# A depthwise convolution whose taps move to TensorE as products over token phases

## The chip, the cores and the metric

The kernel runs on one core of a Trainium2 chip. Its time is the device time of one execution in microseconds. All data are fp32, and the large matrix products are made from a high and a low part in fp32r, three products for one.

## What is computed

The model has eight stages on 512 tokens of 1024 channels: two attention layers, then feed-forward, S5, feed-forward, feed-forward, **convolution**, feed-forward. Only the convolution mixer changes:

```
def layernorm(x, g, b):
    mu = mean(x); var = mean((x - mu)^2)          # over the 1024 channels
    return (x - mu) * rsqrt(var + EPS) * g + b

def conv_mixer(h, w_in, b_in, dw, dw_b, ln_g, ln_b, w_out, b_out):
    z = h @ w_in + b_in                           # 1024 -> 2048
    a, g = split(z, 2)
    z = a * sigmoid(g)
    z = depthwise_conv(z, dw, causal, 31 taps) + dw_b
    z = silu(layernorm(z, ln_g, ln_b))
    return z @ w_out + b_out
```

Every output token of a channel is a sum over 31 earlier tokens of the same channel, with 31 weights of its own.

## The kernel before

Channels lie on the 128 partitions in eight tiles (KD = 8), tokens along the free dimension (T = 512). Each stage is five functions, one for each engine's queue (SP issues the DMAs; PE, ACT, DVE and POOL compute), ordered by semaphores. An engine works its queue strictly in the written order, so a wait holds up all that is behind it.

Weights come in blocks of 256 columns into two slots. `load_block` (L364) waits until the block two before has been split; `split_h` on ACT makes the high part once PE is done with the slot (`mm_done`), `split_l` on DVE the low part (two inputs in SBUF, 128x2048), and then PE may start (`l_done`). `mm3` makes the three products. Each of the four passes `i` of the convolution's input projection uses two blocks, b0+2i (the value half, banks 0 and 1) and b0+2i+1 (the gate half, banks 2 and 3), and gives the tiles 2i and 2i+1: 48 matmuls of 512 columns for a block. `in_pair` is the first pass, tangled with the end of the stage before.

DVE evicts the banks with the factor `rstd` (L1226 and L1233: one operand in PSUM), ACT takes the sigmoid (L1166), and DVE multiplies both (L1237) into `ZP`, which has 30 zero columns ahead of the tokens. The taps of a tile are then divided. On PE (`taps_pe`, L1110) a tap is a product with a diagonal matrix: ACT makes two diagonals for a tap (high and low, L1181) and PE three products of 512 columns, 14 taps for a tile, 17 for the last two. On DVE (`taps_dve`, L1123) a tap is one multiply-add over 512 columns, `CV = CV + w * shifted ZP`, followed by a drain since the next one reads what it wrote. One tap is in ACT's first copy (L1173). `merge` (L1217) adds the bank to `CV`. PE makes the taps of pass i-1 after the projection of pass i. POOL makes the low parts of `ZP` (L1267).

The layer norm follows in one line: POOL sums the eight tiles (L1274), PE sums over partitions with a matrix of ones (L1144), ACT scales the mean (L1185), DVE subtracts it from each tile (L1249), ACT squares (L1190), POOL sums (L455), PE sums over partitions (L1146), ACT takes the root (L1192), DVE the reciprocal (L1251) and the product (L1254), ACT Silu (L1196) and the high part (L1199), DVE the low part (L1257). With the first low part PE begins the output projection (`out_pe`).

Of the kernel before, what the change touches and what calls it, by code (L numbers as in the profile page):

```python
# [7 lines left out]
ALU = mybir.AluOpType  # L8
ACT = mybir.ActivationFunctionType
# [86 lines left out]
def program(nc, io, stages=FULL):  # L96
    ctx = ExitStack()
    with ctx:
# [128 lines left out]
        ZP = sb("ZP", [P, KD, CONV_PAD + T], F32, rb)  # L227
        CV = sb("CV", [P, KD, T], F32, rb)
        SG = sb("SG", [P, 2, T], F32, rb)
        ZH = sb("ZH", [P, KD, CONV_PAD + T], F32R, rb)  # L230
        ZL = sb("ZL", [P, KD, CONV_PAD + T], F32R, rb)
        dwH = sb("dwH", [P, CONV_W * KD], F32R, rb)
        dwL = sb("dwL", [P, CONV_W * KD], F32R, rb)
        DIAGS = 30
        diag = sb("diag", [P, DIAGS, P], F32R, rb)
        YC = ZP[:, :, 0:T]
# [73 lines left out]
        def col(name, k, n=0):  # L310
# [14 lines left out]
            "s5": dict(z=KD, h2=KD, l2=KD, ysq_in=8, ysq_use=6),  # L325
# [768 lines left out]

        def conv_sp(sp, s):
            b0 = first_block[s]
            w = io["cv_w_in_2"][0].rearrange("(k p) n -> p k n", p=P)
            for i in range(4):
                load_block(sp, b0 + 2 * i, 0, raw3(0, KD), w[:, :, i * 256:(i + 1) * 256])
                load_block(sp, b0 + 2 * i + 1, 1, raw3(1, KD), w[:, :, D + i * 256:D + (i + 1) * 256])  # L1100
            out_sp(sp, b0 + 8, io["cv_w_out_2"][0])

        def share(k):
            return 17 if k >= KD - 2 else 14

        TAPS_P = [sum(share(k) for k in range(n)) for n in range(KD + 1)]

        def taps_pe(pe, s, k):  # L1110
            n, acc = share(k), bank[4 + k % 3][:, :]
            pe.wait_ge(ss(s, "zl"), at(s, "zl", k + 1))
            if k >= 3:
                pe.wait_ge(ss(s, "cv"), at(s, "cv", k - 2))
            for t in range(n):
                d = 2 * (TAPS_P[k] + t)
                pe.wait_ge(ss(s, "diag"), at(s, "diag", d + 2))
                high, low = diag[:, d % DIAGS, :], diag[:, (d + 1) % DIAGS, :]
# [4 lines left out]
        def taps_dve(dve, k, t0, t1):  # L1123

            for t in range(t0, t1):
                dve.scalar_tensor_tensor(CV[:, k, :], ZP[:, k, t:t + T], dwT[:, t * KD + k:t * KD + k + 1],  # L1126
                                         CV[:, k, :], ALU.mult, ALU.add)
                dve.drain()

        def conv_pe(pe, s):  # L1130
            b0, j0 = first_block[s], tiles_before[s]
            for i in range(4):
                if i == 0:
                    in_pair(pe, s, b0, j0)
                    continue
                pe_block256(pe, b0 + 2 * i, 0, j0 + 4 * i, XH, XL)
                pe_block256(pe, b0 + 2 * i + 1, 1, j0 + 4 * i + 2, XH, XL)
                if i >= 1:
                    taps_pe(pe, s, 2 * i - 2)
                    taps_pe(pe, s, 2 * i - 1)  # L1140
            taps_pe(pe, s, KD - 2)
            taps_pe(pe, s, KD - 1)
            pe.wait_ge(ss(s, "cvsum"), at(s, "cvsum", KD))
            pe.matmul(stat[:, :], ones[:, :], ssq[:, :], start=True, stop=True).then_inc(ss(s, "cvstat"), 1)  # L1144
            pe.wait_ge(ss(s, "censum"), at(s, "censum", KD))
            pe.matmul(stat[:, :], ones[:, :], ssq[:, :], start=True, stop=True).then_inc(ss(s, "censtat"), 1)  # L1146
            out_pe(pe, s, b0 + 8, j0 + 16, (s, "l2"))

        def conv_act(act, s):
# [6 lines left out]
            act.activation(dwH[:, :], dwT[:, :], ACT.Copy).then_inc(ss(s, "dwh"), 1)  # L1156
            act.wait_ge(ss(s, "dwl"), at(s, "dwl", 1))

            for i in range(4):
# [9 lines left out]
                for k in (2 * i, 2 * i + 1):  # L1169
                    act.wait_ge(ss(s, "z"), at(s, "z", k + 1))  # L1170
                    act.activation(ZH[:, k, :], ZP[:, k, :], ACT.Copy).then_inc(ss(s, "zh"), 1)
                    last = CONV_W - 1
                    act.activation(CV[:, k, :], ZP[:, k, last:last + T], ACT.Identity, bias=col("cv_dw_b_2", k),  # L1173
                                   scale=dwT[:, last * KD + k:last * KD + k + 1]).then_inc(ss(s, "cva"), 1)
                for k in (2 * i, 2 * i + 1):
                    for t in range(share(k)):
                        n = TAPS_P[k] + t
                        if 2 * n >= DIAGS:
                            act.wait_ge(ss(s, "ptap"), at(s, "ptap", n - DIAGS // 2 + 1))
                        for m, part in enumerate((dwH, dwL)):  # L1180
                            act.activation(diag[:, (2 * n + m) % DIAGS, :], ident[:, :], ACT.Copy,  # L1181
                                           scale=part[:, t * KD + k:t * KD + k + 1].bitcast(F32))\
                               .then_inc(ss(s, "diag"), 1)
            act.wait_ge(ss(s, "cvstat"), at(s, "cvstat", 1))
            act.activation(rms[:, :], stat[:, :], ACT.Copy, scale=1.0 / D).then_inc(ss(s, "mu"), 1)  # L1185
            for k in range(KD):
# [1313 lines left out]
```

## Time and profile before

| | |
|---|---|
| time, median of 3 runs | 3062.64 us (3060.99 to 3070.03) |
| the profiled execution | 3068.31 us, of which span 3066.5 us |
| busy: PE, DVE, ACT, POOL | 91%, 54%, 38%, 15% of the span |
| the chain that ended last | PE 76%, DVE 10%, issue 4%, ACT 3% |
| convolution stage | from about 2403 to 2699 us on the profile's clock |
| its taps | PE and DVE, from 2439 to 2585 us |
| its layer norm | to 2622 us |
| mean granted TensorE clock | 0.938 of full speed |

The page tells the share of each engine over the whole span and in 40 slices of 77 us. The convolution fills under four of these, so it is read from questions put to the trace: busy time in stretches, an engine's instructions in order of time, and the groups of instructions of one line. In a row of a timeline the first number is the start in us, the second the length; "x8" behind it means eight instructions merged into one row, from the first start to the last end. A bracket gives the idle time of the engine before it, and what ended it.

### The profile page before, as it was taken

What the parts mean: (1) busy time and instruction counts of PE and PEld (TensorE: products, weight loads), DVE (VectorE), ACT (ScalarE), POOL (GpSimd) and SP (SyncE); (2) the same over time, 40 slices, a digit from 0 to 9 for tenths busy, and PEclk for the clock granted to TensorE, in tenths of its full rate; (3) what the DMA queues carried; (4) which work ended last, traced back from release to release, by engine and by line L of the source; (5) the groups of instructions that cost most, each with busy time, mean ns of one, the idle gap of its engine ahead of it and who ended that gap; (6) DMA issues with size and microseconds to landing.
All of it is one profiled execution on the core that took longest, in us unless ns stands there. A gap on an engine that the chain in (4) does not pass through costs nothing.

```text
span 3066.5 us, 37070 instructions
## 1 busy us (share of the span) xinstructions
PE 2799.9 (91%) x13972; PEld 2299.9 (75%) x13972; DVE 1653.3 (54%) x2427; ACT 1156.3 (38%) x1943; POOL 449.2 (15%) x383
## 2 busy tenths in 40 slices
PE   6987978978979999989699999999999997899998
PEld 5855767845768888888578888888888885788887
DVE  4469755379756543375536443264432697554423
ACT  3237843237834432222324222242222565432222
POOL 1011001020017830024302000010000212200000
PEclk9987989987999999987699999999999998899999
DMA  3320002220014332342222222332223210123222
GB/s 129 96 82 1 1 28 85 97 68 1 1 34 119 132 117 82 99 133 70 64 81 81 85 95 84 95 97 84 94 84 94 83 56 28 56 83 96 87 87 74
DMA packets 292400, 234.80 MB, mean 77 GB/s; under 512 B 43683, under 2 KB 286060, under 8 KB 291756
## 3 DMA queue, kind: packets, MB, share of 16 engines
q1 hardware_dynamic: 289180, 219.49, 23.5%
q10 hardware_dynamic: 2016, 7.46, 0.8%
q0 software_dynamic: 1072, 6.10, 0.6%
q8 instruction: 82, 1.34, 0.2%
q14 instruction: 50, 0.41, 0.0%
HBM read 220.83 MB, written 12.19 MB: 76 GB/s over the span
## 4 chain that ended last, share of the span: by engine, by line
PE 76%; DVE 10%; issue 4%; ACT 3%; DVEq 3%; POOLq 2%; POOL 1%; SPq 0%; DMA 0%; ACTq 0%
PE bank L376 23%; PE bank L378 22%; PE bank L377 22%; DVE WL L362 2%; PE bank L1566 1%; ACT WH L357 1%; DVE stats L1870 1%; PE bank L1553 1%; PE bank L1578 1%; DVE XL L434 1%; DVE CV L1126 1%; POOLq L2318 1%; DVEq L1871 1%; POOLq L2316 1%; DVE E L1897 1%
## 5 line engine op out<-in xcount | busy, mean ns | idle before, releaser
L376 PE MATMUL bank<-XH,WH 128*128 128x512 f32 (+1 forms) x2688 | 996.8, 371 | 79.2 <-DVE WL L362 25.4
L378 PE MATMUL bank<-XH,WL 128*128 128x512 f32 (+1 forms) x2688 | 988.4, 368 | 0.0
L377 PE MATMUL bank<-XL,WH 128*128 128x512 f32 (+1 forms) x2688 | 986.7, 367 | 0.0
L362 DVE TENSOR_TENSOR WL<-raw,WH 128x2048 fp32r<-128x2048 f32 (+1 forms) x212 | 447.8, 2112 | 558.1 <-ACT WH L357 557.7
L376 PEld LDWEIGHTS bank<-XH,WH 128*128 128x128 f32 x2688 | 516.6, 192 | 176.6 <-issue 37.5
L357 ACT ACTIVATE WH<-raw 128x2048 fp32r<-128x2048 f32 (+1 forms) x212 | 370.0, 1746 | 581.6 <-PE bank L378 581.6
L377 PEld LDWEIGHTS bank<-XL,WH 128*128 128x128 f32 x2688 | 517.3, 192 | 90.0 <-issue 1.0
L378 PEld LDWEIGHTS bank<-XH,WL 128*128 128x128 f32 x2688 | 516.1, 192 | 87.8
L378 PE MATMUL bank<-HH,WL 128*128 128x512 f32 (+1 forms) x792 | 293.4, 371 | 0.0
L376 PE MATMUL bank<-HH,WH 128*128 128x512 f32 (+1 forms) x792 | 293.3, 370 | 0.0
L377 PE MATMUL bank<-HL,WH 128*128 128x512 f32 (+1 forms) x792 | 292.7, 370 | 0.0
L976 POOL TENSOR_TENSOR ssq<-ssq,sq 128x512 f32<-128x512 f32 x24 | 31.0, 1292 | 1195.8 <-ACT sq L887 1195.8
L844 ACT ACTIVATE HH<-work 128x512 f32 (+1 forms) x88 | 55.7, 632 | 362.4 <-DVE work L930 362.4
L377 PEld LDWEIGHTS bank<-HL,WH 128*128 128x128 f32 x792 | 148.9, 188 | 28.8
L376 PEld LDWEIGHTS bank<-HH,WH 128*128 128x128 f32 x792 | 148.6, 188 | 28.2
L378 PEld LDWEIGHTS bank<-HH,WL 128*128 128x128 f32 x792 | 148.8, 188 | 27.6
L840 ACT ACTIVATE work<-work 128x512 f32<-128x512 f32 x88 | 55.2, 632 | 270.5 <-DVE work L923 270.5
L928 DVE TENSOR_TENSOR work<-bank,rstd 128x512 f32<-128x512 f32 x88 | 60.8, 690 | 171.7 <-PE bank L378 167.8
L923 DVE TENSOR_TENSOR work<-bank,rstd 128x512 f32<-128x512 f32 x88 | 60.1, 687 | 163.6 <-PE bank L378 154.2
L1712 ACT ACTIVATE E<-bank,stats 128x512 f32<-128x512 f32 (+1 forms) x176 | 113.1, 646 | 47.6 <-DVE stats L1872 36.0
L1870 DVE TENSOR_REDUCE stats<-bank 128x1 f32<-128x512 f32 (+1 forms) x176 | 107.7, 634 | 28.7 <-PE bank L1555 27.5
L1566 PE MATMUL bank<-ident,E 128*128 128x128 f32 x448 | 82.8, 308 | 34.2 <-DVE PTL L1879 31.0
(379 smaller groups left out, 3599.8 us busy)
## 6 DMA issues: line engine op xcount, KB each, us to landing
raw<-in_ffn_w_dram SPq DMA_DIRECT2D x88, 1024.0 KB, 5.3
raw<-in_ffn_w_dram SPq DMA_DIRECT2D x64, 704.0 KB, 4.6
raw<-in_w_in_dram SPq DMA_DIRECT2D x24, 1024.0 KB, 5.2
raw<-in_w_out_dram SPq DMA_DIRECT2D x8, 1024.0 KB, 5.1
raw<-in_cv_w_in_dram SPq DMA_DIRECT2D x8, 1024.0 KB, 5.4
cs_scr<-CSA ACTq DMA_DIRECT2D x8, 520.0 KB, 3.0
raw<-in_w_mem_kv_dram SPq DMA_DIRECT2D x4, 1024.0 KB, 5.4
raw<-in_s_w_in_dram SPq DMA_DIRECT2D x4, 1024.0 KB, 7.7
```

The source lines that it names most:

```text
L357: act.activation(WH[:, slot, 0:n * P], raw[:, slot, 0:n * P], ACT.Copy).then_inc(h_done, 1)
L362: dve.tensor_tensor(WL[:, slot, 0:n * P], raw[:, slot, 0:n * P], WH[:, slot, 0:n * P].bitcast(F32), ALU.subtract).then_inc(l_done, 1)
L376: pe.matmul(out, WH[:, slot, c:c + P], h, start=start, stop=False)
L377: pe.matmul(out, WH[:, slot, c:c + P], l, start=False, stop=False)
L378: return pe.matmul(out, WL[:, slot, c:c + P], h, start=False, stop=stop)
L840: act.activation(work2[:, o, :], work1[:, o, :], ACT.Silu).then_inc(ss(s, "silu"), 1)
L844: act.activation(HH[:, bass.ds(2 * i + o, 1), :], work1[:, o, :], ACT.Copy).then_inc(ss(s, "hh"), 1)
L923: dve.tensor_tensor(work1[:, o, :], bank[o][:, :], rstd[:, :], ALU.mult).then_inc(acc_read, 1)
L928: dve.tensor_tensor(work1[:, o, :], bank[2 + o][:, :], rstd[:, :], ALU.mult).then_inc(acc_read, 1)
L1566: mm = pe.transpose(bank[4 + u % 2][:, c * P:(c + 1) * P], E[:, SCORE0[u] % 6, c * P:(c + 1) * P], ident[:, :])
L1712: act.activation(E[:, m % 6, 0:nk * P], bank[m % 4][:, 0:nk * P], ACT.Exp, bias=stats[:, 1, m % 8:m % 8 + 1], scale=scale, accum_out=stats ...
L1870: dve.tensor_reduce(stats[:, 0, c:c + 1], bank[(m + i) % 4][:, 0:nk * P], AX, ALU.max)
```

## The change

Tiles 0, 1 and 2 (`TILES_D`) stay on DVE, with all of their 31 taps there (one in ACT's first copy, 30 on DVE). Tiles 0 and 1 are done in turns, with a drain only after each pair; `CHUNKS` spreads the 90 taps over the four passes as 14, 16, 16 and 44.

Tiles 3 to 7 (`TILES_P`) go to PE whole. The tokens of such a tile are split in four phases (token = 4n + phase) and its channels in four groups of 32. The gate product is written in phase order into `ZS`; 16 DMAs of 32 partitions x 128 tokens bring it to `PZ`, where the 128 partitions are 4 phases x 32 channels. There the convolution of one group is nine products of 128 rows, 128 output rows and 128 columns, in plain fp32, summed in PSUM: 36 for a tile. Their weight matrices `MM` are made by POOL, half a tile in one operation: the tap table `WT` (broadcast along 32 columns) times a 32x32 identity `EYE` (broadcast along 72), 128x2304 elements out, ten such products in three buffers. ACT fills `WT` and `EYE` with 20 small copies first. A finished tile is evicted by ACT into `PO`, goes back with 16 DMAs into `CP`, and ACT copies it with the bias into `CV`. The 160 DMAs are issued by SP, between the loads of weights.

The layer norm takes a provisional mean from the five tiles that are ready first (0, 1, 3, 4, 5: POOL's sum, then PE and ACT), subtracts it from each tile as the tile comes, squares it on ACT and sums over partitions on PE for each tile. PE also sums the last three centred tiles; that gives the mean that is left, which is taken out of the variance and then out of the tiles (four on DVE, four on POOL). Root and reciprocal become a logarithm and an exponential on ACT. The sum of the provisional mean stands ahead of tile 7's products on PE, and on ACT tile 7's eviction stands behind the first five squares.

The diff, cut to its core:

```diff
@@ taps and queues
+        TILES_D = (0, 1, 2)
+        TILES_P = (3, 4, 5, 6, 7)
+        FIRST = (0, 1, 3, 4, 5)
+        CENTRE = FIRST + (2, 6, 7)
+        TAPS_D = [(k, t) for t in range(CONV_W - 1) for k in (0, 1)] + [(2, t) for t in range(CONV_W - 1)]
+        CHUNKS = (0, 14, 30, 46, len(TAPS_D))
...
         def conv_sp(sp, s):
+            def to_phases(k):
+                n = k - TILES_P[0]
+                sp.wait_ge(ss(s, "z"), at(s, "z", k + 1))
+                if n >= 1:
+                    sp.wait_ge(ss(s, "u_in"), at(s, "u_in", 16 * PH * 4 * n))
+                for g in range(4):
+                    for ph in range(PH):
+                        sp.dma_start(PZ[ph * PW_:(ph + 1) * PW_, n, g, LEAD:], ZS[g * PW_:(g + 1) * PW_, k % 2, ph, :])\
+                          .then_inc(ss(s, "u_in"), 16)
+            def from_phases(k):
+                n = k - TILES_P[0]
+                sp.wait_ge(ss(s, "po"), at(s, "po", n + 1))
+                if n >= 1:
+                    sp.wait_ge(ss(s, "y_out"), at(s, "y_out", 16 * PH * 4 * n))
+                for g in range(4):
+                    for ph in range(PH):
+                        q = PH - 1 - ph
+                        sp.dma_start(CP[g * PW_:(g + 1) * PW_, n, ph, :], PO[q * PW_:(q + 1) * PW_, n % 2, g, :])\
+                          .then_inc(ss(s, "y_out"), 16)
+            for i in range(3):
+                pair(i)
+            to_phases(3)
+            pair(3)
+            to_phases(4)
+            to_phases(5)
+            out_block(0)
+            out_block(1)
+            to_phases(6)
+            to_phases(7)
+            for k in (3, 4, 5):
+                from_phases(k)
+            out_block(2)
+            out_block(3)
+            for k in (6, 7):
+                from_phases(k)
@@ conv_pe
-                pe.matmul(acc, high, ZH[:, k, t:t + T], start=(t == 0), stop=False)
-                pe.matmul(acc, high, ZL[:, k, t:t + T], start=False, stop=False)
-                pe.matmul(acc, low, ZH[:, k, t:t + T], start=False, stop=(t == n - 1)).then_inc(ss(s, "ptap"), 1)
+            for half in range(2):
+                m = 2 * n + half
+                pe.wait_ge(ss(s, "diag"), at(s, "diag", m + 1))
+                for g in (2 * half, 2 * half + 1):
+                    for j in range(9):
+                        c = (g % 2) * NQ + j * PH
+                        mm = pe.matmul(acc[:, g * NS:(g + 1) * NS],
+                                       MM[:, m % 3, c:c + PH, :].rearrange("p q c -> p (q c)"),
+                                       PZ[:, n, g, j:j + NS], start=(j == 0), stop=(j == 8))
+                mm.then_inc(ss(s, "ptap"), 1)
...
+                if i == 2:
+                    taps_pe(pe, s, 3)
+            for k in (4, 5, 6):
+                taps_pe(pe, s, k)
+            pe.wait_ge(ss(s, "cvsum"), at(s, "cvsum", len(FIRST)))
+            pe.matmul(stat[:, :], ones[:, :], ssq[:, :], start=True, stop=True).then_inc(ss(s, "cvstat"), 1)
+            taps_pe(pe, s, 7)
+            for n, k in enumerate(CENTRE):
+                if k not in FIRST:
+                    pe.wait_ge(ss(s, "cen"), at(s, "cen", n + 1))
+                    mm = pe.matmul(bank[6][:, :], ones[:, :], CV[:, k, :], start=(n == len(FIRST)), stop=(n == KD - 1))
+                pe.wait_ge(ss(s, "censq"), at(s, "censq", n + 1))
+                pe.matmul(stat[:, :], ones[:, :], sq[:, n % 2, :], start=(n == 0), stop=(n == KD - 1))\
+                  .then_inc(ss(s, "censtat"), 1)
@@ conv_act
-            act.activation(dwH[:, :], dwT[:, :], ACT.Copy).then_inc(ss(s, "dwh"), 1)
-                        for m, part in enumerate((dwH, dwL)):
-                            act.activation(diag[:, (2 * n + m) % DIAGS, :], ident[:, :], ACT.Copy,
+            for ph in range(PH):
+                rows = slice(ph * PW_, (ph + 1) * PW_)
+                act.activation(EYE[rows, :], ident[rows, rows], ACT.Copy)
+                for g in range(4):
+                    ins = act.activation(WT[rows, :, g, 5 - ph:5 - ph + CONV_W], taps[g * PW_:(g + 1) * PW_, TILES_P[0]:, :],
+                                         ACT.Copy)
+            ins.then_inc(ss(s, "wt"), 1)
...
+            evict(3)
+            evict(4)
+            back(3)
+            evict(5)
+            back(4)
+            evict(6)
+            back(5)
             act.wait_ge(ss(s, "cvstat"), at(s, "cvstat", 1))
+            act.activation(rms[:, :], stat[:, :], ACT.Copy, scale=1.0 / (P * len(FIRST))).then_inc(ss(s, "mu"), 1)
+            for n in range(len(FIRST)):
+                square_c(n)
+            evict(7)
+            square_c(5)
+            back(6)
+            square_c(6)
+            back(7)
+            square_c(7)
@@ conv_dve
+            def taps(i):
+                for n in range(CHUNKS[i], CHUNKS[i + 1]):
+                    k, t = TAPS_D[n]
...
+                    ins = dve.scalar_tensor_tensor(CV[:, k, :], ZP[:, k, t:t + T], dwT[:, t * KD + k:t * KD + k + 1],
+                                                   CV[:, k, :], ALU.mult, ALU.add)
...
+                    if k:
+                        dve.drain()
...
+            for n in range(KD):
+                centre(n)
+            dve.wait_ge(ss(s, "mu"), at(s, "mu", 2))
+            dve.wait_ge(ss(s, "censtat"), at(s, "censtat", KD))
+            dve.scalar_tensor_tensor(work2[:, 0, :], stat[:, :], 1.0 / D, work1[:, 1, :], ALU.mult, ALU.subtract)\
+               .then_inc(ss(s, "var"), 1)
+            for k in range(4):
+                dve.tensor_tensor(CV[:, k, :], CV[:, k, :], work1[:, 0, :], ALU.subtract)
@@ conv_pool
+            def matrices(m):
+                n, half = m // 2, m % 2
+                shape = [P, 2 * NQ, PW_]
+                if m >= 3:
+                    pool.wait_ge(ss(s, "ptap"), at(s, "ptap", m - 2))
+                w = WT[:, n, 2 * half:2 * half + 2, :].rearrange("p g q -> p (g q)")
+                pool.tensor_tensor(MM[:, m % 3], w.unsqueeze(2).to_broadcast(shape),
+                                   EYE[:, :].unsqueeze(1).to_broadcast(shape), ALU.mult).then_inc(ss(s, "diag"), 1)
...
+            for m in range(8):
+                matrices(m)
+            add(0)
+            add(1)
+            matrices(8)
+            add(2)
+            add(3)
+            matrices(9)
+            add(4)
+            pool.wait_ge(ss(s, "mu"), at(s, "mu", 2))
+            for k in range(4, KD):
+                pool.tensor_tensor(CV[:, k, :], CV[:, k, :], work1[:, 0, :], ALU.subtract).then_inc(ss(s, "csub"), 1)
```

## Rows read from the trace of the kernel before

**Rows 1.** busy time by stretch: us, then busy us (count) per engine, clock, DMA

```profile
2431.00:2584.70 153.70, 149.99 (x642) 120.53 (x642) 136.11 (x161) 102.64 (x268) 28.20 (x14) 1.00 0.16 51
2584.70:2615.10 30.40, 4.15 (x5) 1.03 (x5) 18.69 (x20) 13.65 (x19) 12.94 (x9) 0.51 0.00 0
```

**Rows 2.** DVE's timeline, 2551 to 2585: start, us, engine, line, operation, count, idle

```profile
2551.58 1.28 DVE L1233 TENSOR_TENSOR work<-bank,rstd 128x512 f32<-128x512 f32 x2
...
2557.68 1.28 DVE L1219 TENSOR_TENSOR CV<-CV,bank 128x512 f32<-128x512 f32 x2
2558.88 24.96 DVE L1126 SCALAR_TENSOR_TENSOR CV<-ZP,dwT,CV 128x512 f32<-128x512 f32 x26
2583.92 1.29 DVE L1219 TENSOR_TENSOR CV<-CV,bank 128x512 f32<-128x512 f32 x2
```

**Rows 3.** timelines of PE, DVE and ACT in the layer norm

```profile
2587.41 2.08 PE L1144 MATMUL bank<-ssq,ones 128*128 128x512 f32 x2 [4.39 <-POOL ssq L1274]
...
2611.55 0.80 ACT L1196 ACTIVATE CV<-CV,vecT 128x512 f32<-128x512 f32 x1
...
2612.92 0.80 ACT L1196 ACTIVATE CV<-CV,vecT 128x512 f32<-128x512 f32 x1
...
2621.25 0.69 DVE L1257 TENSOR_TENSOR XL<-CV,XH 128x512 fp32r<-128x512 f32 x1 [0.68 <-ACT XH L1199]
```

**Rows 4.** timelines of ACT and DVE at the start of the convolution

```profile
2429.59 0.40 ACT L1156 ACTIVATE dwH<-dwT 128x248 fp32r<-128x248 f32 x1
2432.39 1.28 ACT L1166 ACT_TABLE_LOAD   x1 [2.39 <-DVE work L1233]
...
2434.44 1.41 DVE L1237 SCALAR_TENSOR_TENSOR ZP<-work,vecT,SG 128x512 f32<-128x512 f32 x2 [1.53 <-ACT SG L1166]
2436.86 2.29 DVE L362 TENSOR_TENSOR WL<-raw,WH 128x2048 fp32r<-128x2048 f32 x1 [1.00 <-ACT WH L357]
```

**Rows 5.** PE's timeline: starts at full clock, and eight fp32 records of 128 columns

```profile
2441.15 0.39 PE L376 MATMUL bank<-XH,WH 128*128 128x512 f32 x1
...
2442.08 0.39 PE L377 MATMUL bank<-XL,WH 128*128 128x512 f32 x1
...
2428.01 1.05 PE L478 MATMUL bank<-ident,rcol 128*128 128x128 f32 x8
```

**Rows 6.** granted clock of a stretch, and two starts inside it

```profile
2615.00:2619.00 4.00, 3.90 (x9) 3.15 (x10) 2.94 (x5) 3.90 (x7) 0.00 (x0) 0.50 0.00 0
...
2615.66 0.63 PE L377 MATMUL bank<-XL,WH 128*128 128x512 f32 x1
2616.09 0.63 PE L378 MATMUL bank<-XH,WL 128*128 128x512 f32 x1
```

**Rows 7.** timelines of POOL and DVE in an earlier feed-forward stage

```profile
964.55 1.95 POOL L738 TENSOR_TENSOR tabA<-tabA,par 128x1024 f32<-128x1024 f32 x1
966.45 4.00 POOL L739 TENSOR_TENSOR tabA<-tabA,par 128x1024 f32<-128x1024 f32 x1
...
965.22 3.43 DVE L362 TENSOR_TENSOR WL<-raw,WH 128x2048 fp32r<-128x2048 f32 x1 [2.50 <-ACT WH L357]
968.57 0.68 DVE L928 TENSOR_TENSOR work<-bank,rstd 128x512 f32<-128x512 f32 x1
969.33 1.65 DVE L930 TENSOR_TENSOR work<-work 128x512 f32<-128x512 f32 x1
```

**Rows 8.** DVE's timeline in the centring, and the first tap

```profile
2592.56 1.75 DVE L1249 TENSOR_TENSOR CV<-CV,rms 128x512 f32<-128x512 f32 x1
...
2439.07 1.85 DVE L1126 SCALAR_TENSOR_TENSOR CV<-ZP,dwT,CV 128x512 f32<-128x512 f32 x1
```

**Rows 9.** POOL's product of two plain inputs of 1024

```profile
973.22 2.40 POOL L742 TENSOR_TENSOR tabA<-tabA,bt 128x1024 f32<-128x1024 f32 x1
```

**Rows 10.** SyncE's timeline in the s5 stage, and its DMA issues by line

```profile
1342.66 3.88 SPq L1980 DMA_DIRECT2D u_scr<-sq  x8
...
y_scr<-YS SPq DMA_DIRECT2D x64, 32.0 KB, 1.9
```

More of the change, by code:

```diff
@@ L1097, in conv_sp, with pair @@
             w = io["cv_w_in_2"][0].rearrange("(k p) n -> p k n", p=P)
-            for i in range(4):
+            wo = io["cv_w_out_2"][0].rearrange("(k p) n -> p k n", p=P)
+            def pair(i):
                 load_block(sp, b0 + 2 * i, 0, raw3(0, KD), w[:, :, i * 256:(i + 1) * 256])
                 load_block(sp, b0 + 2 * i + 1, 1, raw3(1, KD), w[:, :, D + i * 256:D + (i + 1) * 256])
-            out_sp(sp, b0 + 8, io["cv_w_out_2"][0])
-        def share(k):
-            return 17 if k >= KD - 2 else 14
@@ L1123, in taps_dve, with out_block @@
[L1123 to L1128, printed above, removed]
+            def out_block(i):
+                load_block(sp, b0 + 8 + i, i % 2, raw3(i % 2, KD), wo[:, :, i * 256:(i + 1) * 256])
+            def to_phases(k):
[7 more added lines that the diff above has]
+                          .then_inc(ss(s, "u_in"), 16)
@@ L1184, in conv_act @@
-            act.wait_ge(ss(s, "cvstat"), at(s, "cvstat", 1))
-            act.activation(rms[:, :], stat[:, :], ACT.Copy, scale=1.0 / D).then_inc(ss(s, "mu"), 1)
-            for k in range(KD):
-                act.wait_ge(ss(s, "cen"), at(s, "cen", k + 1))
-                if k >= 2:
-                    act.wait_ge(ss(s, "censum"), at(s, "censum", k - 1))
-                act.activation(square_to(k), CV[:, k, :], ACT.Square).then_inc(ss(s, "censq"), 1)
-            act.wait_ge(ss(s, "censtat"), at(s, "censtat", 1))
@@ new lines, in conv_act @@
+            square_c(7)
+            act.wait_ge(ss(s, "censum"), at(s, "censum", 1))
+            act.activation(work1[:, 0, :], bank[6][:, :], ACT.Copy, scale=1.0 / D)
+            act.activation(work1[:, 1, :], bank[6][:, :], ACT.Square, scale=1.0 / D).then_inc(ss(s, "mu"), 1)
+            act.wait_ge(ss(s, "var"), at(s, "var", 1))
+            act.activation(work2[:, 0, :], work2[:, 0, :], ACT.Ln, bias=eps_c[:, 0:1]).then_inc(ss(s, "sigma"), 1)
+            act.wait_ge(ss(s, "sigma"), at(s, "sigma", 1))
@@ L1258, in conv_dve @@
                    .then_inc(ss(s, "l2"), 1)
+            for k in range(KD):
+                if k >= 4:
+                    dve.wait_ge(ss(s, "csub"), at(s, "csub", k - 3))
+                dve.tensor_tensor(CV[:, k, :], CV[:, k, :], rms[:, :], ALU.mult).then_inc(ss(s, "nrm"), 1)
+                if k >= 2:
+                    low(k - 2)
+            low(KD - 2)
+            low(KD - 1)
             out_dve(dve, s, b0 + 8, j0 + 16, s0 + 16, YC, post, lambda o: col("cv_b_out_2", o))
@@ new lines, in add @@
+            def add(n):
+                k = FIRST[n]
+                if k in TILES_D:
+                    pool.wait_ge(ss(s, "cv"), at(s, "cv", k + 1))
+                else:
+                    pool.wait_ge(ss(s, "cvb"), at(s, "cvb", k - TILES_P[0] + 1))
+                if n == 0:
+                    ins = pool.tensor_copy(ssq[:, :], CV[:, k, :])
+                else:
+                    ins = pool.tensor_tensor(ssq[:, :], ssq[:, :], CV[:, k, :], ALU.add)
+                ins.then_inc(ss(s, "cvsum"), 1)
+                pool.wait_ge(ss(s, "cvsum"), at(s, "cvsum", n + 1))
```

174 lines of the change are left out of this document (87 added, 87 removed).

## The prediction

> **What bounds the kernel now.** I read the page first, then busy time by stretch, then the timelines of DVE, ACT and PE around the convolution, and last the chain of waits behind it. All times below are on the clock of the profiled execution before (span 3066.5 us, 3068.3 us in all); the median of its runs is 3062.6, and I put differences on that median. The page shows PE busy for 91% of the span, so elsewhere in the kernel nothing that this change touches can matter. In the convolution there are two stretches [rows 1]. From 2431 to 2585 PE (150 of 154 us) and DVE (136) are both full: TensorE does 118 taps as three fp32r products each, VectorE 122 taps at 0.83 us each and the evictions [rows 2]. From 2585 to 2615 PE does 4 us of work: that is the layer norm's serial chain, sum, mean, centring, squares summed on POOL, root, reciprocal, and then a 1.37 us rhythm of Silu and copy on ACT [rows 3]. The next matmuls need the eight lows of the result; the last is ready at 2621.25 + 0.69 = 2621.9. From there both kernels do the same work, so the question is: when is that eighth low ready afterwards?
>
> **Matmuls.** TensorE loses 354 products of 0.233 us (four starts in 0.93 [rows 5]), 82.5 us. It gains five tiles of 36 fp32 products of 128 columns. Eight instruction records of just that shape take 1.05 us [rows 5]: at most 0.131 from start to start, and 0.111 when the last one's tail is taken off, which I use. An fp32 product leaves two records, so a tile is 72 x 0.111 = 8.0 us (9.4 at most) and the five are 40. After 10 us of PE idle time the granted clock was 0.50 of full speed (1.2 GHz) for the 4.0 us from 2615 on, with 0.43 us between starts instead of 0.233 [rows 6]: such a return costs some 1.9 us.
>
> **VectorE's own work.** 122 taps and 8 merges become 90 taps. Tiles 0 and 1 alternate and drain once per pair. Two undrained operations of this kind start 0.66 us apart (1.41 - 0.75 [rows 4]), a drained one takes 0.83, so 30 pairs cost 44.7 and tile 2 24.8: some 70 us, against 107.
>
> **The shared port, the term that decides.** POOL now makes ten weight products of 128x2304 with both inputs read in SBUF. What such an operation does to DVE is seen far from here: while POOL's L738 (128x1024, one input broadcast) ran from 964.55, a split on DVE that began at 965.22 took 3.43 us instead of 2.29; L739, issued at 966.45, then took 4.00 instead of 1.95; and L930 behind it 1.65 instead of 0.69. The DVE eviction between them, with one operand in PSUM, took its usual 0.68 [rows 7]. So two-SBUF-input work on DVE and work on POOL exclude each other, an instruction at a time. They take turns: in the centring DVE operations take 1.75 us, 1.06 of it a wait for POOL's 512-element sum; the first tap took 1.85 in place of 0.75 [rows 8]. The Trainium skill (SBUF — State Buffer, Who interferes with whom) has the rule behind it, that a DVE instruction with two SBUF inputs and a GpSimd instruction that reads SBUF exclude each other and the later one "fully blocks". By that rule, which speaks against this change, a tap waits for a whole product; were the port only shared out, the sum would be nearer the first rival below. The trace agrees with the rule (3.43 and 1.65 us).
>
> How long is one product? L739 held DVE until about 970.3, from 968.5, 1.8 us for 1024 elements [rows 7]. In proportion 2304 take 4.1 us, which I use: same kind, one input broadcast. The least is 3.8 (if part of the 1.8 is fixed). The most is from L742 with two plain inputs, 2.40 us of which some 0.1 is start-up, 2.25 x 2304/1024 = 5.1 [rows 9].
>
> **The start.** ACT's conversion of the taps (0.40 us [rows 4]) becomes 20 small copies of 32 partitions. At most 0.40 each is 8, at least 0.2 is 4; I take 6.0, ending 2435.7. POOL's first product starts there. The table load and two sigmoids follow (to 2438.3), and ACT's split of the second block of weights ends 2440.1. On DVE two gate operations and a split, all with two SBUF inputs, now take turns with three products: product to 2439.9, gate to 2440.6, product to 2444.7, gate to 2445.4, product to 2449.5, split to 2451.7. In the kernel before it ended at 2439.15 [rows 4], and PE needs it at 2431.3 + 48 x 0.233 = 2442.5. PE stalls 9.2 us and comes back at the lower clock, 1.9 more. VectorE then does 14 taps (10.4), two evictions and a split before the next pair can begin, 0.7 after PE is free. So the last of the projections ends at 2431.3 + 3 x 22.4 + 8.0 (tile 3) + 9.2 + 1.9 + 0.7 = 2518.3.
>
> **To the end of the taps.** From the evictions of that pair to the taps DVE needed 6.1 us (2551.58 to 2557.68 [rows 2]); so they start at 2524.4. 14 paired taps and 30 single ones are 10.4 + 24.8. Against them stand five products (5 to 9), each free to start only as PE uses up earlier ones, and five sums: 5 x 4.1 + 5 x 1.06 = 25.8. End: 2585.4, where before it was 2585.2 (2583.92 + 1.29 [rows 2]). So PE and DVE each lose about 40 us of work, and the port gives it back.
>
> **The queue of SyncE.** 160 transfers join it. Eight of the nearest kind are issued in 3.88 us, so 0.47 each, and land 1.9 us after [rows 10]: 16 are 7.6 + 1.8 = 9.4 us. Ahead of the loads of the output weights now stand tiles 4 and 5: the first load leaves near 2507 and lands 5.4 later, 2512.4, and DVE comes to its split near 2516. After gate 6 (2521) come tiles 6 and 7 out and 3, 4, 5 back, 45 us, to 2566; then a sum, the provisional mean, and tile 7 on PE, done near 2578. That hides under the taps with 14 us to spare counted to ACT's eviction of tile 7, because ACT does five squares first.
>
> **The tail.** After the last tap: centre and square 1.4, three sums of squares on PE, at the lower clock as L1144 had after 4 us idle (two records in 2.08 [rows 3], some 0.4 of it tail, so 1.7 us apart, later 1.4) 4.7, and the fifth square 0.5: 6.6. Eviction and 16 transfers: 9.6. Copy back, centre, two fp32 products at 1.7, variance: 5.6. Four subtractions on DVE in turns with POOL's four: 5.5, and they hide ACT's logarithm and exponential. Multiply, Silu, copy, low: 2.9; seven more at 1.37: 9.6. In all 39.8, against 2621.9 - 2585.2 = 36.7. The eighth low comes at 2625.2, 3.3 us later than before: 3066 us. With products of 3.8 to 5.1, copies of 4 to 8 us and a clock at either level throughout, the likeliest case spans -6 to +9: 3057 to 3072.
>
> **Rivals.** (1) The products cost DVE little, because POOL gets these broadcast reads through faster or DVE slips taps in. For it: DVE and PE have really lost 40 us of work; against it, rows 7 and 8. Without stalls the pairs end at 2507 and the taps near 2550, and SyncE becomes the bound: gate 6 at 2510.6, 45.2 us of transfers, 3.8 for copy, sum and mean, 9.9 for tile 7, 10.0 for its eviction and way back, then 5.6 + 2.4 + 2.9 + 9.6: 2600. That is 22 us less, 3041; at half the stalls, about 3050. (2) A product is as dear as a plain one, 5.1 us: three at the start and five at the end at 1.0 more each, and the tail unchanged: +8, 3074. It decides for slower from some 4.9 us a product. The Trainium skill (GPSIMD Engine Reference, Elementwise — side-by-side cycle accounting) gives 4497 ns for a plain 2048-element `tensor_tensor`; an estimate from that page is 5.06 us for 2304 and a time of 3074. (3) SyncE's queue is the bound: 80 transfers between gate 6 and the mean have 14 us to spare, so from 0.65 us a transfer. At 0.8 it is 80 x 0.15 + 16 x 0.33, some 17 us more, 3083. Rows 10 speak against it, but those transfers run to DRAM, these from one partition group of SBUF to another.
>
> **Chances.** A measurement can tell about 0.3%, 9 us: faster is below 3053.4, slower above 3071.8. Likeliest case 0.52 (0.05 faster, 0.43 same, 0.04 slower); rival 1 0.22, all faster; rival 2 0.18 (0.03 same, 0.15 slower); rival 3 0.08 (0.02 same, 0.06 slower). Faster 0.27, same 0.48, slower 0.25. The range reaches to most of rivals 1 and 2 and leaves out about 0.1 on each side: 3045 to 3079.
>
> **What would show it.** Right: product records on POOL of 4 us and more; about five taps of some 4.9 us on DVE; the second block of the projections 9 us late with a granted clock of half behind it; the last tap near 2585; ACT's eviction of tile 7 after the fifth square. Rival 1: taps all near 0.8, PE waiting for POOL's sum before tile 7. Rival 2: products of 5 us or more. Rival 3: SyncE issuing without a pause beyond 2580, and copies back late. What would make it wrong: a product time outside 3.8 to 5.1, DVE passing POOL twice in a row, or transfers that take another time than those to DRAM.

## The result, and the profile after

The change makes the kernel slower: 3088.6 us (median of 4 runs, 3084.3 to 3092.3) against 3064.6 for the kernel before on the same chip (3061.0 to 3070.0), a ratio of 1.0076 (1.0055 to 1.0097). The prediction was 3066, with 3079 as its upper end, and a chance of 0.25 for slower. The profiled execution took 3084.3 us, of which 3082.5 are span.

The start of the convolution moves by up to 13 us between executions of the same code in the stages before it, and from the eighth low part to the end every profiled execution takes 444.5 to 444.6 us. So every comparison below uses one measure inside the stage: from the start of ACT's `rstd` (2429.10 before, 2421.37 after) to the end of the eighth low part (2621.94 and 2637.97). Before it is **192.8 us**, after **216.6**: +23.8, where the medians differ by 24.0. Each such number comes from one profiled execution; the ratios come from all. Positions written "at 159" are us after the start of `rstd`.

Busy time after, in two stretches (us; busy us and count of PE, PEld, DVE, ACT, POOL; clock; DMA share; GB/s): from `rstd` to the last tap on DVE, and from there to the eighth low part.

```profile
2421.37:2580.70 159.33, 105.70 (x588) 90.73 (x586) 134.97 (x121) 35.39 (x46) 52.00 (x14) 0.84 0.17 52
2580.70:2637.97 57.27, 30.91 (x117) 18.47 (x117) 22.06 (x29) 26.56 (x36) 7.54 (x5) 0.76 0.16 48
```

PE is busy for 106 us of the first stretch where it was for 150 [rows 1], and DVE is nearly as full as it was (135 us busy, 136 before), through its turns with POOL: its last tap comes at 159.3 where the last merge before came at 156.1. So the first stretch costs 3 us and the second, 57.3 long where it was 36.7, costs 20.5. The second one is on DVE's timeline:

```profile
2576.66 4.04 DVE L1308 SCALAR_TENSOR_TENSOR CV<-ZP,dwT,CV 128x512 f32<-128x512 f32 x1 [0.43 <-issue]
2589.57 3.70 DVE L1352 TENSOR_TENSOR CV<-CV,rms 128x512 f32<-128x512 f32 x6 [8.87 <-ACT rms L1270]
2603.65 0.69 DVE L1352 TENSOR_TENSOR CV<-CV,rms 128x512 f32<-128x512 f32 x1 [10.37 <-ACT CV L1237]
2614.49 0.69 DVE L1352 TENSOR_TENSOR CV<-CV,rms 128x512 f32<-128x512 f32 x1 [10.14 <-ACT CV L1237]
2618.86 0.69 DVE L1359 SCALAR_TENSOR_TENSOR work<-bank,work 128x512 f32<-128x512 f32 x1 [3.68 <-PE bank L1205]
2619.47 5.92 DVE L1362 TENSOR_TENSOR CV<-CV,work 128x512 f32<-128x512 f32 x4
```

The taps are done and the mean is not there: 8.87 us. Then DVE waits twice for a tile on its way back. Three of the longest waits from 2425 us on (engine and line, what it waited for, us, times, longest):

```profile
ACT CV L1237 <- DMA CP<-PO: 60.9, 4, 33.3
...
PE bank L1196 <- POOL ssq L1406: 37.2, 1, 37.2
...
ACT WH L360 <- DMA raw<-in_cv_w_out_dram: 26.7, 1, 26.7
```

TensorE stood 37.2 us before tile 7 for GpSimd's sum, the sum stood for ACT's copies back, and those for their transfers. SyncE's timeline says why:

```profile
2463.29 10.11 SPq L1134 DMA_DIRECT2D PZ<-ZS  x16
2473.44 1.21 SPq L371 DMA_DIRECT2D raw<-in_cv_w_in_dram  x2
2487.71 22.32 SPq L1134 DMA_DIRECT2D PZ<-ZS  x32
2510.07 1.21 SPq L371 DMA_DIRECT2D raw<-in_cv_w_out_dram  x2
2528.47 21.76 SPq L1134 DMA_DIRECT2D PZ<-ZS  x32
2550.27 32.78 SPq L1146 DMA_DIRECT2D CP<-PO  x48
2583.09 1.21 SPq L371 DMA_DIRECT2D raw<-in_cv_w_out_dram  x2
2584.40 27.62 SPq L1146 DMA_DIRECT2D CP<-PO  x32
```

16 transfers take 10.11 us to issue, 0.63 each, where [rows 10] had 0.47. From 2528.5 to 2583.1 SyncE issues set after set; the only pauses, up to 1.3 us, are for the set before to land. The load of block b0+8 leaves only at 2510.07, at 88.7, behind the transfers of tiles 4 and 5; ACT waits 26.7 us for it. So gate 6 (the product of value and gate half of tile 6, L1324) starts at 103.6 and, in turns with a product of POOL, ends at 107.1.

### The profile page after: what moved, and what is told of

Read it like the earlier page. It is cut to its first block, busy times and chain, and to the rows that moved or that the text cites. A ratio compares the mean times of both kernels' runs of the same rounds, so it can differ in the third digit from the quotient of the medians.

```text
span 3082.5 us, 36962 instructions
## 1 busy us (share of the span) xinstructions
PE 2768.4 (90%) x13998; PEld 2274.3 (74%) x13998; DVE 1653.5 (54%) x2390; ACT 1094.8 (36%) x1727; POOL 469.5 (15%) x381
## 4 chain that ended last, share of the span: by engine, by line
PE 72%; DVE 10%; issue 4%; ACT 4%; DVEq 3%; SPq 3%; POOLq 2%; DMA 1%; POOL 1%; ACTq 0%
PE bank L379 21%; PE bank L380 21%; PE bank L381 21%; DVE WL L365 2%; SPq L1134 2%; PE bank L1710 1%; ACT WH L360 1%; SPq L1146 1%; DVE stats L2014 1%; PE bank L1697 1%; DVE XL L437 1%; PE bank L1722 1%; DVE work L534 1%; DVE X L538 1%; POOLq L2462 1%
## 5 line engine op out<-in xcount | busy, mean ns | idle before, releaser
L365 DVE TENSOR_TENSOR WL<-raw,WH 128x2048 fp32r<-128x2048 f32 (+1 forms) x212 | 459.7, 2169 | 561.4 <-ACT WH L360 561.0
L448 POOL TENSOR_TENSOR ssq<-ssq,sq 128x256 f32<-128x256 f32 x112 | 96.4, 860 | 118.4 <-ACT sq L428 112.8
```

What stands on the lines that cost most here:

```text
L365: dve.tensor_tensor(WL[:, slot, 0:n * P], raw[:, slot, 0:n * P], WH[:, slot, 0:n * P].bitcast(F32), ALU.subtract).then_inc(l_done, 1)
L448: ins = pool.tensor_tensor(ssq[:, HALF[h]], ssq[:, HALF[h]], sq[:, k % 2, HALF[h]], ALU.add)
```

## The experiments

Two theories at the start. **Q**: two chains end almost together, VectorE's with the port lock, and SyncE's queue of transfers, and the queue is the later one. **L**: the port lock is the whole loss. The first kernel cuts the products to a ninth (of this and the next diffs only the core is shown):

```diff
-                shape = [P, 2 * NQ, PW_]
+                shape = [P, 8, PW_]
```

> The changed kernel with each of POOL's ten weight products cut from 128x2304 to 128x256 elements (the other weights stay zero, so the convolution of tiles 3 to 7 is left unfinished); everything else, the 160 transfers too, is as in the change. Measure: from the eviction of the first statistic (rstd) to the end of the eighth low, 192.8 us before and 216.6 after. Theory Q (two chains end almost together, SyncE's queue of transfers last): the three stalls by products go, gates 6 and 7 come some 13 us earlier and with them the sum ahead of tile 7, but PE still waits for that sum long after the taps are done; 14 us less, 202 to 203. Theory L (the port lock is the whole loss): 25 us less or more, 190, below the kernel before.

Measured: 199.9 us; ratio to before 1.0009 (0.9997 to 1.0021). With no long hold of the port left, the stage is still 7 us slower than before, where L wanted 190; Q had 202 to 203. The taps end 27 us earlier, at 132.1, and the same wait is longer:

```profile
2582.10 3.70 DVE L1352 TENSOR_TENSOR CV<-CV,rms 128x512 f32<-128x512 f32 x6 [19.61 <-ACT rms L1270]
```

L falls as the whole cause. The queue moves up by 17 us too, since the stall at the start and the turns of the splits delay the gates that feed it.

Loads ahead of transfers:

```diff
-            to_phases(4)
-            to_phases(5)
             out_block(0)
+            to_phases(4)
             out_block(1)
+            to_phases(5)
```

> The changed kernel with the load of the first output block ahead of tile 4's transfers and the second ahead of tile 5's, nothing else. Theory Q: the split that waited for the load until 2515.6 can begin some 6 us earlier, the last pass and gates 6 and 7 follow, and so does all of SyncE's chain: 7 us less, 209 to 211. Theory L: the taps on DVE stay where they were and the end moves by less than 2 us.

Measured: 205.6; ratio 1.0044 (1.0030 to 1.0057). 11.0 us come back for two loads moved, more than the 6 to 8 expected: gate 6 starts at 93.0 instead of 103.6, and what stands behind it moves up by 11 to 12.

The price of a transfer by itself, put into the kernel before (SyncE's timeline; in order: 32x512 B between SBUF buffers across groups of 32 partitions; the same within a group; to DRAM; to DRAM in pieces of 256 B while loads run; four of 64 KB; four of 128x512 B):

> The kernel before with six batches of transfers of scratch data on SyncE's queue during the projection (and 20 instead of 30 buffers for diagonals, to make room). It measures the disputed cost by itself: start to start of issues on SyncE. In the change it was 0.63 us for 32 partitions x 512 bytes from SBUF to SBUF, against 0.47 for the S5 stage's SBUF to DRAM. If it is the crossing of partition groups, only the first batch shows 0.63; if it is SBUF as the target, the first two, the batch of four-times-larger and of 128 partitions too; if it is the shape of 32 rows of 512 bytes, the batch to DRAM with this shape too, and the one in S5's shape (16 rows in eight pieces of 256 bytes) 0.47.

```profile
2424.61 10.36 SPq L1114 DMA_DIRECT2D PB<-PA  x16
2436.19 10.66 SPq L1120 DMA_DIRECT2D PB<-PA  x16
2448.07 7.31 SPq L1126 DMA_DIRECT2D p_scr<-PA  x16
...
2456.52 9.00 SPq L1133 DMA_DIRECT2D q_scr<-PA  x16
2466.93 2.61 SPq L1139 DMA_DIRECT2D PB<-PA  x4
2472.22 2.48 SPq L1144 DMA_DIRECT2D PB<-PA  x4
```

0.65 and 0.67 us each from SBUF to SBUF, crossing or not; 0.46 to DRAM, 0.56 there in small pieces beside loads; and 0.65 and 0.62 from SBUF to SBUF for four times the bytes. The dear ones have SBUF at both ends, whatever their size up to 64 KB. Which end costs is not shown: the transfers from DRAM into SBUF in the kernel with the hop by way of DRAM, below, lasted 0.34 to 0.60 us each.

Returns issued by ACT instead of SyncE (the `sp.` calls of `from_phases` become `act.`, each set behind its eviction):

> The changed kernel with the 80 returning transfers issued by ACT behind each eviction, and the 80 outgoing ones still by SyncE. Theory Q: the returns of tiles 3 and 4 no longer queue behind tiles 6 and 7, the sum ahead of tile 7 comes some 13 to 20 us earlier, then the end of the taps on DVE (2580.7) is what the first centring waits for: 5 to 9 us less, 208 to 212. Theory L: 2 us less at most.

Measured: 214.9; ratio 1.0051 (1.0032 to 1.0070). The expected 208 to 212 were missed. ACT's timeline shows one cause:

```profile
2541.52 10.36 ACTq L1219 DMA_DIRECT2D CP<-PO  x16
2551.93 0.60 ACT L1227 ACTIVATE PO<-bank 128x512 f32<-128x512 f32 x1 [10.44 <-issue]
2553.13 11.89 ACTq L1219 DMA_DIRECT2D CP<-PO  x16
```

ACT pays the same price, and its next eviction and copy stand behind it for 10 us. The other cause is chance. Gate 6, which this edit does not reach, came 4 us later, because gate 4 began 0.5 us later (65.6 against 65.1), met a product of POOL and took 4.9 us in place of 1.2. The gates of tiles 4 and 5, in after and here:

```profile
2486.46 6.11 DVE L1324 SCALAR_TENSOR_TENSOR ZS<-work,vecT,SG 128x512 f32<-128x512 f32 x2 [0.19 <-ACT SG L1253]
...
2496.64 9.81 DVE L1325 SCALAR_TENSOR_TENSOR ZS<-work,vecT,SG 128x512 f32<-128x512 f32 x2 [0.19 <-ACT SG L1249]
```

So a single stage number of a kernel with POOL's products can be off by some 4 us. The returns of tile 3 are still 6 us earlier (at 134) and the mean 4.6. The ratio, whose interval overlaps after's, doesn't settle what this edit is worth.

Light products and loads first, together:

> After with both of the edits of the two kernels before it: GpSimd's products are cut to 128x256 (most of the convolution of tiles 3 to 7 is left out: its matrices are wrong), and SyncE issues the load of block b0+8 ahead of tile 4's transfers and that of b0+9 ahead of tile 5's. Measured from the start of rstd to the end of the eighth low part, after takes 216.6 us, light products alone 199.9 (16.7 less), loads alone 205.6 (11.0 less). If the products and the transfer queue bind in the same places (the wait of the split of b0+8, the sixth gate), what both give together is less than the 27.8 us that they sum to: my reckoning of the queue gives 193 to 196 us (21 to 24 less). If they add up, 189. If the products were the only cause and the loads merely repaired what they had delayed, the loads add nothing: 199 to 200. Kernel: 193 to 196 is 3062 to 3067 us.

Measured: 195.9, inside the 193 to 196; ratio 1.0020 (1.0006 to 1.0033). The two gains of 16.7 and 11.0 make 20.7, not 27.8: both shorten one path, the one to gate 6. DVE's wait for the mean is still 20.11 us. With neither long products nor the loads in the way the stage is still 3 us slower than before, and the mean, which comes through the queue, is what DVE waits for.

The queue itself. Each set of 16 is replaced by four transfers to DRAM and one of 256 KB back:

```diff
-                    for ph in range(PH):
-                        sp.dma_start(PZ[ph * PW_:(ph + 1) * PW_, n, g, LEAD:], ZS[g * PW_:(g + 1) * PW_, k % 2, ph, :])
+                    sp.dma_start(z_scr[n, :, :, g].rearrange("q c s -> c q s"), ZS[g * PW_:(g + 1) * PW_, k % 2])
+                sp.wait_ge(ss(s, "u_in"), at(s, "u_in", HOP * n + 64))
+                sp.dma_start(PZ[:, n, :, LEAD:], z_scr[n].rearrange("q c g s -> (q c) g s"))
```

> After, with each set of 16 transfers replaced by four to a DRAM buffer and one of 256 KB back from it (same rows, same places), so SyncE issues 5 transfers for a tile in place of 16, products as they are. Theory Q (the issue of 16 transfers at 0.63 us, 10.1 us of SyncE a set, is what the end waits for): a set takes 4 x 0.46 + 0.65 of issue and 1.9 of landing in between, about 4.5 us, the load of b0+8 is issued about 11 us earlier, the fifth sum no longer ends last, the taps on VectorE do (they end 156 to 159 after rstd), evict 7 behind the five squares at 166, eighth low 198 to 200: 16 to 18 us less than after's 216.6, kernel 3068 to 3072. Theory L (the shared port alone): the products and their stalls stay, less than 4 us change. If the extra hop costs more than it saves (landing of 2 to 3 us twice for every tile on the path of gates 5 to 8), 216 or more.

Measured: 192.8; ratio 1.0004 (0.9991 to 1.0016). All 23.8 us are gone, more than the 16 to 18 expected, with every product and its lock still there. SyncE and DVE:

```profile
2463.27 1.79 SPq L1136 DMA_DIRECT2D z_scr<-ZS  x4
2466.41 0.60 SPq L1139 DMA_DIRECT2D PZ<-z_scr  x1
...
2515.05 1.79 SPq L1136 DMA_DIRECT2D z_scr<-ZS  x4
2518.18 0.53 SPq L1139 DMA_DIRECT2D PZ<-z_scr  x1
...
2575.55 0.75 DVE L1313 SCALAR_TENSOR_TENSOR CV<-ZP,dwT,CV 128x512 f32<-128x512 f32 x1 [0.43 <-issue]
2576.47 3.70 DVE L1357 TENSOR_TENSOR CV<-CV,rms 128x512 f32<-128x512 f32 x6 [0.16 <-DVE CV L1313]
```

An outgoing set takes 3.6 to 3.7 us with the hop, a returning one 3.4 to 7.1. Tile 7's way back, from SyncE's first issue to ACT's copy, takes 6.1 us where it took 11.3. The sum ends at 135, the centring follows the last tap after 0.16 us, and the last tap comes at 154.9. (The products only had other things to collide with: the split of b0+8 took 2.3 us here and 6.0 in after.)

To show that it is the issuing and not the route, eleven transfers that nobody uses are put in front of each set of five:

```diff
+                for j in range(11):
+                    g, ph = j // 4, j % 4
+                    sp.dma_start(PD[ph * PW_:(ph + 1) * PW_, g, 8:], ident[g * PW_:(g + 1) * PW_, :])
```

> The kernel with the hop by way of DRAM (f2, 192.8 us from rstd to the eighth low part against after's 216.6), with eleven transfers of 32x512 B from a constant to a buffer that nobody reads put in front of each set of five, so that SyncE issues 16 for a tile again. If it is SyncE's time of issue that costs after its 23.8 us, a set takes 11 x 0.63 + 4.5 = 11.4 us here, as much as after's 10.1 + 1.8 with its landing, and the measure goes back to 214 to 219 us (kernel 3086 to 3091). If the hop helped by something else (transfers to other partition groups being slow, an earlier landing), the idle ones cost little: 193 to 200.

Measured: 224.7; ratio 1.0115 (1.0098 to 1.0133), higher than the 214 to 219 expected:

```profile
2545.07 6.85 SPq L1135 DMA_DIRECT2D PD<-ident  x11
2551.97 2.04 SPq L1148 DMA_DIRECT2D z_scr<-ZS  x4
2555.36 0.58 SPq L1151 DMA_DIRECT2D PZ<-z_scr  x1
...
2608.32 3.70 DVE L1370 TENSOR_TENSOR CV<-CV,rms 128x512 f32<-128x512 f32 x6 [19.15 <-ACT rms L1288]
```

10.9 us a set, and the wait for the mean is back, while DVE's last tap stayed at 155.2. So of the 32 us against the kernel with the hop some 28 hang on SyncE's time of issue alone; the other 4 come by way of the port, gate 4 having met a product (4.5 us in place of 1.2), as in the kernel with returns on ACT. These 4 are also half of the 8 us above after; the rest is that each set lands later than after's, behind its second hop.

The port by itself: the ten products computed by DVE, between its taps (`pool.tensor_tensor` becomes `dve.tensor_tensor`, three from tap 15 on, seven among the last 44).

> After, with the ten products of 128x2304 computed by VectorE itself, between its taps (three from tap 15 on, seven among the last 44), GpSimd keeps only the sums, queue and layer norm as they are. From the subtraction of 128x2048 (2.29 us) and a tap (0.66 for 512) a product should take 2.6 to 3.0 us of VectorE, 26 to 30 us in all; GpSimd's hold the shared port 43.9 us, of which VectorE was seen to lose some 28. Theory: a product costs the kernel less on VectorE than on GpSimd, the split of b0+3 ends at 13 to 14 after rstd in place of 24.8 and the wait of TensorE of 11.9 us goes; taps end at 155 to 160; the transfer queue sets the rest: 199 to 205 us, kernel 3068 to 3075. Rival: VectorE's own work was already last and the product costs it as much as the lock did: 213 or more.

Measured: 206.7; ratio 1.0061 (1.0041 to 1.0082); the upper end was 205. The stall at the start shrinks from 11.9 to 3.5 us, and a product takes DVE 2.56 us where one of GpSimd's holds the port for 4.1 to 4.4. But the taps end at 156.3, 3 us earlier only: DVE pays with its own time (25.6 us for the ten) most of what it no longer loses.

The layer norm alone, put into the kernel before (mean of the first five tiles, squares summed on TensorE, second mean, Ln and Exp):

> The kernel before with the new layer norm alone: mean of the first five tiles, found while TensorE runs the taps of tile 7, centring by it behind the last merge, squares and their sum on TensorE, mean of the centred values and its subtraction (four tiles on VectorE, four on GpSimd), Ln and Exp for the root. The convolution is before's. Before takes 36.7 us from the last merge (156.1) to the eighth low part (192.8). Here the centring starts at once (two waits for sum and mean less, some 5 us), the root costs two table loads in place of one and no reciprocal, and the subtractions take 6 us: from 31 to 34 us, so 187 to 190 us in all, kernel 3057 to 3061. If the added subtraction and the table loads eat it, 192 to 196.

Measured: 186.7; ratio 0.9984 (0.9972 to 0.9997). From the last merge (155.5) to the eighth low part 31.2 us, before 36.7. This part of the change is a gain of 5.5 us; it is the convolution with its transfers that eats it.

Order alone: loads first, as above, and on ACT the eviction of tile 7 ahead of the five squares:

```diff
+            evict(7)
             for n in range(len(FIRST)):
                 square_c(n)
-            evict(7)
-            square_c(5)
             back(6)
+            square_c(5)
```

> After with the order of instructions changed and nothing else: load of b0+8 ahead of tile 4's transfers, of b0+9 ahead of tile 5's (alone 205.6 us, 11.0 less than after), and on ScalarE evict 7 ahead of the five squares and back 6 right behind them. The eviction of tile 7 should come as soon as TensorE's taps of tile 7 end, 162 to 163 after rstd in place of 169.0, its 16 returns end at 173, the eighth centring moves up by the same 6 to 7 us: 198 to 200 us, kernel 3067 to 3072. If the squares, now later, become last, 203 or more.

Measured: 202.4; ratio 1.0046 (1.0030 to 1.0063). That is neither the 198 to 200 nor the 203 or more. Eviction 7 came at 165.9, not 163: TensorE's products of tile 7 began behind 38.18 us of idle time and took 9.8 us, at a granted clock of 0.83 on average, where two tiles took 16.2 at 1.00 in after. The eighth centring moved up by 3 us, half of what was expected.

**A version that beats both kernels.** First products on DVE, five transfers a set, loads first and eviction 7 first:

> After with four edits: products on VectorE, five transfers by way of DRAM for each set of 16, load of b0+8 ahead of tile 4's transfers and of b0+9 ahead of tile 5's, evict 7 ahead of the five squares. If three causes (port, transfers, evict 7 behind the squares) each hold up the stage, all of them gone gives: taps end 152 to 157 (VectorE's own work is the bound), centring at once, eighth centring 8 to 10 us later, tail of 25: 184 to 190 us, that is 3 to 9 us under before's 192.8; kernel 3056 to 3062. If VectorE's 26 us of products undo it: 195 or more.

Measured: 180.4; 3057.1 us, ratio 0.9964 (0.9951 to 0.9978); faster than expected, the last tap being at 145.5. In its trace ACT copied tile 7 back 17 us after its transfers had been issued, behind the squares, and four subtractions on DVE in turns with four on POOL took 6.3 us. So the backs were put ahead of the squares, and all eight subtractions on DVE:

> The version with products on VectorE, five transfers a set, loads first and evict 7 first (f4: 180.4 us, 3057), with two edits more: backs 6 and 7 ahead of all squares on ScalarE (in f4 the returns of tile 7 had landed some 13 us before the back that used them), and the second mean subtracted from all eight tiles by VectorE (in f4 four and four took turns with GpSimd's, 6.3 us). Centrings: eight in a row behind the taps (145.5 to 150.5), last square's matmul at about 158 in place of 160.5, subtractions 4.9 in place of 6.3: 176 to 178 us, kernel 3052 to 3055. If the eight squares, one after another between ScalarE and TensorE, are what binds and not the backs: 179 to 180.

Measured: 177.1; 3050.1 us against 3067.7 on that chip, ratio **0.9958** (0.9943 to 0.9974), 15.7 us less than before in the stage. DVE now goes from the taps straight into all eight centrings; what is left of the waits is 8.56 us for the squares:

```profile
2561.19 4.88 DVE L1325 SCALAR_TENSOR_TENSOR CV<-ZP,dwT,CV 128x512 f32<-128x512 f32 x6 [0.44 <-issue]
2566.23 4.90 DVE L1369 TENSOR_TENSOR CV<-CV,rms 128x512 f32<-128x512 f32 x8 [0.16 <-DVE CV L1325]
2579.69 0.69 DVE L1376 SCALAR_TENSOR_TENSOR work<-bank,work 128x512 f32<-128x512 f32 x1 [8.56 <-ACT work L1283]
2580.30 4.89 DVE L1379 TENSOR_TENSOR CV<-CV,work 128x512 f32<-128x512 f32 x8
```

Eight subtractions by one engine take 4.89 us, where four beside four of the other took 5.92 (last row of DVE in after). Which of the edits gives what between the 192.8 us with the hop alone and this 177.1 was not taken apart.

## Why the prediction was wrong

**Right: the port.** A product took 4.08 us with the port free (the first) and 4.39 between taps, where 4.1 was used, and a tap behind it 4.04. The turns at the start, timelines of POOL, DVE and PE of after:

```profile
2430.99 13.02 POOL L1394 TENSOR_TENSOR MM<-WT,EYE 128x2304 f32<-128x2304 f32 x3 [15.78 <-ACT WT L1222]
...
2432.99 7.10 DVE L1320 SCALAR_TENSOR_TENSOR ZP<-work,vecT,SG 128x512 f32<-128x512 f32 x2 [8.50 <-ACT SG L1253]
2440.01 6.15 DVE L365 TENSOR_TENSOR WL<-raw,WH 128x2048 fp32r<-128x2048 f32 x1
...
2446.22 0.79 PE L379 MATMUL bank<-XH,WH 128*128 128x512 f32 x1 [11.93 <-DVE WL L365]
```

PE stalls 11.93 us where 9.2 was predicted: the products started at 9.6 after `rstd` and not at 6.6, since the 20 small copies on ACT took 0.45 us each on average (the 16 larger 0.51), where 0.30 was used. It comes back at a granted clock of 0.50 with 0.43 between starts, as in [rows 6]. The last tap, predicted at 156.3 on this measure (2585.4 - 2429.1), came at 159.3. That it is so near is in part luck. The last 44 taps were to run from 95.3 to 156.3, with five products and five sums against them; they began 18.7 us later, at 114.1, and took 45.3 us in place of 61.0. Held back by the queue, they met only two products, and the others fell on splits and gates before them. In the kernel with five transfers a set, where the queue is not in the way, the same taps ran from 97.3 to 154.9, 57.6 us in all, five of them 4.4 to 4.6 us long: there the reckoning holds. DVE in after, then in that kernel:

```profile
2535.42 40.81 DVE L1308 SCALAR_TENSOR_TENSOR CV<-ZP,dwT,CV 128x512 f32<-128x512 f32 x43
...
2518.72 56.41 DVE L1313 SCALAR_TENSOR_TENSOR CV<-ZP,dwT,CV 128x512 f32<-128x512 f32 x43
```

Rivals 1 and 2 fall: DVE did not slip in, and a product does not cost 5.1.

**Wrong: the step on SyncE's queue.** It put tile 7's products on PE done near 2578, that is 149, with "14 us to spare" before the tile's eviction at 163 (2585.4 + 6.6), and so let the queue's chain cost nothing. The products were done at 176.7, and the eviction came at 180.0. The 27.7 us to the products are:
- +15.2 to the end of gate 6 (107.1 against 91.9). The load of b0+8 left at 88.7 and not at 78. The 32 transfers ahead of it took 22.3 us where 2 x 9.4 = 18.8 were reckoned, and they began 7.2 later than the prediction has it, behind a stall that was 2.7 longer and behind gate 4, which tile 3's 16 transfers held back too: a load left behind them, ACT waited 16.30 us for it and DVE 3.44 for ACT. Then the split of b0+8 and the gates took turns with products (6.0 us for the split, 8.4 for the two gates).
- +10.8 from there to the copy back of tile 5 (55.8 against 45): 80 transfers at 0.63 instead of 0.47 are 12.8, and the waits for landings came to 2 less.
- +1.7 from there to the end of tile 7's products (13.8 against 12).

The eviction is 17.1 later than forecast: 3.0 for the taps, 8.9 for the mean, and 5.2 more for the centrings and five squares. The prediction let ACT do the squares while TensorE was free; but with the mean late, tile 7 and the sums of squares want TensorE in the same 9 us, ACT's third square waits 7.44 for it, and the eviction stands behind:

```profile
2598.98 0.63 ACT L1244 ACTIVATE sq<-CV 128x512 f32<-128x512 f32 x1 [7.44 <-PE bank L1205]
...
2601.42 0.58 ACT L1231 ACTIVATE PO<-bank 128x512 f32<-128x512 f32 x1
...
2613.26 1.19 ACT L1237 ACTIVATE CV<-CP,vecT 128x512 f32<-128x512 f32 x1 [8.26 <-DMA CP<-PO]
```

**The tail, term by term.** 39.8 was predicted, 57.3 measured: 8.9 of wait for the mean (0), 11.9 to the eviction (6.6), 11.8 for it and its way back (9.6), 6.3 to the variance (5.6), 5.9 for the subtractions (5.5), 12.5 for the rest (12.5). With the 3.0 at the taps that is 20.5 above the prediction's +3.3, so all 23.8.

**Rival 3 was the case, and was priced wrongly.** It named the mechanism, the place and the doubt (transfers to DRAM against transfers between partition groups), then put the turning point at 0.65 us a transfer and gave it 0.08. At 0.63 the queue was already last. The turning point counted only the 80 transfers behind gate 6 against a fixed 14 us; the sets ahead of gate 6 delay that gate too, so the price is paid on the 32 transfers of tiles 4 and 5, in part on tile 3's 16, on 80 behind the gate and on 16 for tile 7, and the 14 us took every other term at its predicted size. The doubt was also put in the wrong property: crossing groups costs nothing (0.65 against 0.67), and transfers with SBUF at both ends are the dear ones.

What each cause is worth can't be given as shares of a sum, since they meet on one path: without the queue 23.8 us come back, without the long products 16.7, with the loads first 11.0. Not tried: the queue repaired with the products left out, the products alone in the kernel before, and the queue repaired with loads and eviction moved but the products left on POOL.

## What to carry to other kernels

Count the instructions that an issuing queue gets, times the price of that kind with those two ends, and follow them from the first to be issued: a load behind them is late as well, and so is the gate that feeds the next set. A chain that is "hidden with 14 us to spare" on terms taken from a neighbouring kind of row is a rival with a real chance, not 0.08. To reorder a tile across partitions, four transfers to DRAM and one back (3.7 us of the queue, the wait between them included) beat sixteen direct ones (10.1).

## What was not expected of the hardware

- A transfer from SBUF to SBUF took SyncE 0.62 to 0.67 us, of 16 KB or of 64 KB alike, one from SBUF to DRAM mostly 0.45 to 0.47, 0.56 in small pieces beside loads. On ACT 16 from SBUF to SBUF took 10.1 to 11.9 us.
- A product of 128x2304 with both inputs broadcast took GpSimd 4.08 us with the port free, 4.39 between taps, and VectorE 2.56 us.
- Ln and then Exp on ACT took two table loads, and Silu a third (timeline of ACT in after). The Trainium skill (ScalarE: Activation LUTs, Table sets) says that one table set has both Ln and Exp and that the two in a row need one load; the trace differs, and decides:

```profile
2618.45 1.28 ACT L1283 ACT_TABLE_LOAD   x1
...
2620.48 1.28 ACT L1285 ACT_TABLE_LOAD   x1
```

Here they cost nothing, as DVE's subtractions last longer.
